# A decoder layer on one core: output projection with five matmuls a chunk, summed by VectorE, and a reordered opening

## The chip, the cores and the metric

The kernel is one launch on one core of a Trainium2 chip. Its time is the device time of that core in microseconds (us); smaller is better. A core has TensorE (PE, matmuls, with a weight load, PEld, beside each), VectorE (DVE), ScalarE (ACT), GpSimd (POOL) and SyncE (SP, which here only issues DMAs). Each engine takes its instructions in order, and they wait for each other by semaphores.

## The reference

One layer for 512 prompt tokens and 8 x 4 sample tokens, 544 tokens in all, width 2048:

```python
def _combine(x, a, p, ga, gb, w_out, ln_g, ln_b):
    mixed = jnp.concatenate([a.reshape(B, T, ATTN_WIDTH) * jax.nn.silu(ga), p * jax.nn.silu(gb)], axis=-1)
    h = (DEEPNORM_ALPHA * x + jnp.einsum('btc,cd->btd', mixed, w_out)).astype(jnp.float32)
    mu = jnp.mean(h, axis=-1, keepdims=True)
    var = jnp.mean(jnp.square(h - mu), axis=-1, keepdims=True)
    y = (h - mu) * lax.rsqrt(var + LN_EPS) * ln_g.astype(jnp.float32) + ln_b.astype(jnp.float32)
```

Ahead of it one input projection (7248 columns) feeds an indexer that picks the keys, sparse attention `a` for prompt and samples (those over paged caches), and a causal pooling mixer `p`. Everything is float32.

## The kernel before, in words

**Projections.** A float32 product is made from float32r parts: activations are kept as `actH` (rounded) and `actL` (the rest), weights as `wH` and `wL`. ScalarE makes a high part by a copy (`high`), GpSimd the low part by a subtraction (`low`). A tile is 128 output columns, its weights come in two units of 8 chunks (128 rows each) through 4 slots. For each chunk TensorE (`unit`, L1157 to L1175) does wH x actH, wH x actL and wL x actH, each for two halves of 272 tokens in two PSUM banks: six matmuls, and a weight load for each. A tile lies in `acc[0]` or `acc[1]`, two banks each; ScalarE copies it to SBUF (`acc_copied` counts that).

**Opening.** x comes by four DMAs of 1 MB (SP issues tokens 0 to 255, ScalarE the rest and the 32 sample rows). TensorE transposes each token tile in four quarters through four PSUM banks, ScalarE writes `actH` from a bank (L718), VectorE `actL` (L1782). After all five tiles, the 80 columns for the indexer's key and weights are projected (tile 0), then eight query tiles of the indexer from `TILE_A` on.

**Middle.** Value, gate, key and query tiles with the prompt's attention, then four rounds (`group`) in which pooling channels are projected while the samples' keys and values pass through. SP's queue is an order written out by hand. `pool_loads` brings the history rows (`hist`) and `w_pool`, `mask` the list of dropped keys into `probS`, `value_page` and `key_unit` the cache pages. `history` on TensorE transposes `hist`, `probs_turned` the softmaxed `probS`.

**Output projection.** 16 tiles from `TILE_D` on. The first (`first_tile`, L1509) is interleaved with the end of the last round. Tiles 1 to 11 are `unit` again, the last four are done in two parts (`out_part`, 288 and 256 tokens, one matmul per product). When a tile is done and copied to `raw`, `rows` (L1675) transposes it into two banks `yp` and `ys`, in the middle of the next tile. VectorE then adds alpha x + bank into `y` (`residual`), takes statistics and multiplies by `ln_g`. `y` is filled with x by five DMAs, issued once the last attention output has left its bank; behind them in the same queue comes `ln_g` for all partitions. On VectorE the statement ahead of the loop over tiles is: `memset gb`, which waits for all of `y`, then a wait for `ln_g`.

Of the kernel before, what the change touches and what calls it, by code (L numbers as in the profile page):

```python
# [32 lines left out]
P = 128  # L33
D = 2048
KC = D // P
# [49 lines left out]
LATE_T = 2 * P  # L85
EARLY_COLS, LATE_COLS = slice(LATE_T, T), slice(0, LATE_T)
# [24 lines left out]
def tile_turn(tile, i=None, per=0):  # L111
# [8 lines left out]
    return Turn(slot, n if i is None else i * step + n)  # L120

# [53 lines left out]
def layer_program(nc, x_prompt, x_sample, cache_k, cache_v, cache_kidx, state_pool, page_table,  # L175
# [4 lines left out]
    with ctx:  # L180
# [10 lines left out]
        actH = sb("actH", [P, KC, T], F32R)  # L191
        actL = sb("actL", [P, KC, T], F32R)
# [121 lines left out]
        acc_copied = sems("acc_copied", 2)  # L314
        bank_full = {j: sem(f"bank_full{j}") for j in (*four, OUT, SIDE)}
# [63 lines left out]
        xb = banks.stage([f"x{t}{q}" for t in range(TT + 1) for q in range(4)], four)  # L379
# [69 lines left out]
        def _(sp):  # L449
# [15 lines left out]
            sp.dma_start(pageT[:], page_table.rearrange("(a b) c -> a (b c)", a=1)).then_inc(pages_in, 16)  # L465
            sp.dma_start(s_pool[0, :, 0:HIST - NT, :], state_pool[0, :, NT:HIST, :]).then_inc(spool_sent, 16)
# [16 lines left out]
            with sp.Fori(0, 4) as i:  # L483
                for j in range(2):
                    load_tile(w_view, QI0 + (2 * i + j) * P, TILE_A + j, i, 2)

                    for q in range(4):
                        b = xb(f"x{TT}{q}")
                        sp.wait_ge(bank_free[b.slot], b.read)
                    for p in range(BESIDE):  # L490
                        index_page(2 * BESIDE * i + (BESIDE * j + p))
            for j in range(2):
                load_tile(w_view, V0 + j * P, TILE_C + j)
            with sp.Fori(8 * BESIDE, NB * PAGES) as at:
                index_page(at)
# [97 lines left out]
            pool_loads(0)  # L593
# [82 lines left out]
        def _(act):  # L676
# [17 lines left out]

            def halves(ap):
                return ap.rearrange("p (a t) -> p a t", a=2)
# [9 lines left out]
            act.dma_start(headrot[:], head_rot).then_inc(consts_in, 16)  # L706
            act.dma_start(halfscale[:], pool_scale[0].rearrange("(j p) -> p j", p=P), allow_slow_non_contiguous=True).then_inc(consts_in, 16)


            for t in range(TT + 1):  # L710
                if t == TT:
                    for half in range(2):
                        high(0, half, width=KW)
# [7 lines left out]
            for q in range(4):  # L721
                b = xb(f"x{TT}{q}")
                act.wait_ge(bank_free[b.slot], b.read)
            act.dma_start(irot[:], idx_rot).then_inc(irot_in, 16)

# [3 lines left out]
            src, copied = projected(0)  # L729
            act.activation(halves(wiT[ID:KW, :]), src[ID:KW], ACT.Copy, scale=ISCALE)  # L730
            act.activation(halves(kiT[0:ID, :]), src[0:ID], ACT.Copy).then_inc(copied, 1)
# [366 lines left out]
            with act.Fori(0, 5) as i:  # L1098
                for j in range(2):
                    high(TILE_D + j + 2, 0, i, 2)  # L1100
                    src, copied = projected(TILE_D + j, i, 2)
                    act.activation(halves(raw[:, j]), src, ACT.Copy).then_inc(copied, 1)
                    high(TILE_D + j + 2, 1, i, 2)

            def out_copy(n):
                src, copied = projected(TILE_D + n)
                if n < WHOLE:
                    act.activation(halves(raw[:, n % 2]), src, ACT.Copy).then_inc(copied, 1)
# [26 lines left out]
        def _(pe):  # L1135

            for s in (*stage_ready, *stage_free, *acc_copied, *bank_free.values(), *v_free):
                pe.sem_inc(s, 1)
# [1258 lines left out]
```

## Time and profile before

| | us |
|---|---|
| timed runs | 1153.33, 1153.55, 1156.03 (median 1153.55) |
| profiled execution, its own time | 1152.01 |
| its span, first to last instruction | 1150.2 |
| TensorE busy in the span | 1123.2 |
| VectorE, ScalarE, GpSimd busy | 641.5, 327.1, 372.8 |

The span begins with the first instruction, and all moments below count from there. "Idle before" in a row is the time that the engine stood still ahead of the group, and the arrow names what ended it. Matmuls overlap: the distance between starts is what one costs, not its own duration. PEclk 1.00 is full speed (2.4 GHz), 0.50 the lower level (1.2 GHz).

### The profile page before, as it was taken

What the parts mean: (1) busy time and instruction counts of PE and PEld (TensorE: products, weight loads), DVE (VectorE), ACT (ScalarE), POOL (GpSimd) and SP (SyncE); (2) the same over time, 40 slices, a digit from 0 to 9 for tenths busy, and PEclk for the clock granted to TensorE, in tenths of its full rate; (3) what the DMA queues carried; (4) which work ended last, traced back from release to release, by engine and by line L of the source; (5) the groups of instructions that cost most, each with busy time, mean ns of one, the idle gap of its engine ahead of it and who ended that gap; (6) DMA issues with size and microseconds to landing.
All of it is one profiled execution on the core that took longest, in us unless ns stands there. A gap on an engine that the chain in (4) does not pass through costs nothing.

```text
span 1150.2 us, 29683 instructions
## 1 busy us (share of the span) xinstructions
PE 1123.2 (98%) x11836; PEld 1046.7 (91%) x11836; DVE 641.5 (56%) x1184; ACT 327.1 (28%) x605; POOL 372.8 (32%) x158
## 2 busy tenths in 40 slices
PE   6999999999999999999999999999999999999996
PEld 5988889999999999999999898988889889999994
DVE  3566666897547456654266564565546443233356
ACT  5233234323332322332233221221212332121340
POOL 2332332233234333333431313221322233433570
PEclk9999999999999999999999999999999999999997
DMA  8543232333233233335323888887978785232333
GB/s 261 137 108 88 61 100 70 83 93 93 74 91 90 82 86 93 89 83 167 111 66 110 274 318 294 303 284 266 336 240 300 224 284 142 73 91 80 106 108 156
DMA packets 208039, 175.86 MB, mean 153 GB/s; under 512 B 20114, under 2 KB 188874, under 8 KB 206706
## 3 DMA queue, kind: packets, MB, share of 16 engines
q1 hardware_dynamic: 194394, 165.58, 46.7%
q10 hardware_dynamic: 13536, 8.68, 2.5%
q8 instruction: 87, 1.43, 0.5%
q14 instruction: 22, 0.18, 0.0%
HBM read 164.29 MB, written 10.03 MB: 152 GB/s over the span
## 4 chain that ended last, share of the span: by engine, by line
PE 90%; DVE 5%; DMA 1%; issue 1%; SPq 1%; ACT 1%; ACTq 0%; DVEq 0%
PE acc L1173 68%; PE acc L1155 4%; PE acc L1563 3%; PE bank L1494 2%; PE bank L1249 2%; PE bank L1366 2%; PE acc L1616 2%; PE bank L1385 1%; DVE scoreP L1868 1%; DVE top L1864 1%; PE acc L1522 1%; DMA xnat<-in_x_prompt 1%; PE bank L1301 1%; PE bank L1375 1%; DMA hist<-in_state_pool 1%
## 5 line engine op out<-in xcount | busy, mean ns | idle before, releaser
L664 POOL TENSOR_TENSOR wL<-rawW,wH 128x1024 fp32r<-128x1024 f32 (+1 forms) x154 | 372.6, 2421 | 746.7 <-ACT wH L686 746.7
L1173 PE MATMUL acc<-actH,wH 128*128 128x272 f32 (+1 forms) x2168 | 464.2, 295 | 1.2 <-DVE actL L1782 1.2
L1173 PE MATMUL acc<-actH,wL 128*128 128x272 f32 (+1 forms) x2168 | 449.0, 289 | 0.0
L1173 PE MATMUL acc<-actL,wH 128*128 128x272 f32 (+1 forms) x2168 | 447.7, 288 | 0.0
L1173 PEld LDWEIGHTS acc<-actH,wH 128*128 128x128 f32 (+1 forms) x2168 | 339.3, 188 | 31.3 <-issue 29.6
L1173 PEld LDWEIGHTS acc<-actL,wH 128*128 128x128 f32 (+1 forms) x2168 | 340.4, 188 | 0.0
L1173 PEld LDWEIGHTS acc<-actH,wL 128*128 128x128 f32 (+1 forms) x2168 | 338.5, 188 | 0.0
L686 ACT ACTIVATE wH<-rawW 128x1024 fp32r<-128x1024 f32 (+1 forms) x154 | 161.7, 1054 | 262.1 <-PE acc L1173 232.5
L1820 DVE SCALAR_TENSOR_TENSOR scoreP<-relu,wiN,scoreP 128x256 f32<-128x256 f32 (+2 forms) x54 | 45.3, 878 | 33.4 <-ACT relu L743 33.4
L1973 DVE STREAM_TRANSPOSE kPage<-kPage 128x1024 f32<-128x1024 f32 x30 | 37.1, 1238 | 38.2 <-DMA kPage<-in_cache_k 37.4
L2216 DVE SCALAR_TENSOR_TENSOR y<-y,bank 128x512 f32 x12 | 8.2, 688 | 89.8 <-PE bank L1683 86.7
L2030 DVE SCALAR_TENSOR_TENSOR mixed<-bank,gate 128x128 f32<-128x128 f32 x32 | 9.3, 289 | 68.3 <-PE bank L1385 68.3
L743 ACT ACTIVATE relu<-bank 128x512 f32<-128x512 f32 (+3 forms) x63 | 28.9, 502 | 57.8 <-PE bank L1249 34.7
L1905 DVE MAX8 top<-scoreS 32x8 f32<-32x1056 f32 x32 | 39.9, 1247 | 3.1
L1908 DVE MATCH_REPLACE8 scoreS<-top,scoreS 32x1056 f32<-32x1056 f32 x32 | 39.4, 1231 | 0.0
L1563 PE MATMUL acc<-vPage,probST 128*4 128x128 f32 x1024 | 38.5, 273 | 0.4 <-issue 0.4
L1155 PE MATMUL acc<-actH,wH 128*128 128x288 f32 (+1 forms) x128 | 37.8, 295 | 0.0
L1155 PE MATMUL acc<-actL,wH 128*128 128x288 f32 (+1 forms) x128 | 36.9, 288 | 0.0
L1155 PE MATMUL acc<-actH,wL 128*128 128x288 f32 (+1 forms) x128 | 36.8, 287 | 0.0
L1974 DVE STREAM_TRANSPOSE kPage<-kPage 128x1024 f32<-128x1024 f32 x30 | 36.1, 1202 | 0.0
L1494 PE MATMUL bank<-kPage,qBlock 128*32 128x64 f32 x1920 | 33.2, 220 | 0.5 <-issue 0.4
L1563 PEld LDWEIGHTS acc<-vPage,probST 128*4 128x4 f32 x1024 | 23.0, 86 | 10.2 <-issue 8.2
(232 smaller groups left out, 1083.6 us busy)
## 6 DMA issues: line engine op xcount, KB each, us to landing
rawW<-in_w_in SPq DMA_DIRECT2D x112, 512.0 KB, 3.9
vPage<-in_cache_v SPq DMA_DIRECT2D x64, 512.0 KB, 6.7
kPage<-in_cache_k SPq DMA_DIRECT2D x60, 512.0 KB, 5.1
rawW<-in_w_out SPq DMA_DIRECT2D x40, 512.0 KB, 3.9
y<-in_x_prompt SPq DMA_DIRECT2D x4, 1024.0 KB, 7.9
out_y_prompt<-y SPq DMA_DIRECT2D x8, 512.0 KB, 2.6
xnat<-in_x_prompt SPq DMA_DIRECT2D x2, 1024.0 KB, 7.7
xnat<-in_x_prompt ACTq DMA_DIRECT2D x2, 1024.0 KB, 11.4
```

The costliest lines, as they stand in the source:

```text
L664: pool.tensor_tensor(wL[:, slot, :, 0:width], rawW[:, slot, :, 0:width], wH[:, slot, :, 0:width].bitcast(F32), ALU.subtract).then_inc(stag ...
L686: act.activation(wH[:, t.slot, :, 0:width], rawW[:, t.slot, :, 0:width], ACT.Copy).then_inc(high_ready[t.slot], 1)
L743: act.activation(relu[0:rows, t.slot, 0:n], src[0:rows, 0:n], ACT.Relu).then_inc(relu_full[t.slot], 1)
L1155: last = pe.matmul(acc[t.slot][:, e, 0:cols.stop - cols.start], w[:, u.slot, k, :], a[:, (1 - half) * HU + k, cols], start=(half == 0 and ...
L1173: last = pe.matmul(acc[t.slot][0:width, e, 0:HT], w[:, u.slot, k, 0:width], a[:, kk, e * HT:(e + 1) * HT], start=(half == 0 and k == 0 and ...
L1494: last = pe.matmul(bank[b.slot][j * SPAN:(j + 1) * SPAN, at:at + w], qBlock[:, q:q + SPAN], keys[:, :, row:row + STREAK], start=(a == 0 an ...
L1563: return pe.matmul(bank[o.slot][j * SPAN:j * SPAN + NT, a * P:(a + 1) * P], probs, values, start=start and a == 0, stop=stop and a == HALF ...
L1820: dve.scalar_tensor_tensor(sc, relu[:, r.slot, 0:(t + 1) * P], wiN[:, t - 1, ds(h, 1)], sc, ALU.mult, ALU.add).then_inc(bank_free[b.slot], 1)
L1905: own.step(dve.max(top, scores))
L1908: own.step(dve.match_replace(scores, top, scores, PICKED))
L1973: dve.transpose(parts[0], parts[0])
L1974: dve.transpose(parts[1], parts[1]).then_inc(k_turned, 1)
```

## The change

1. `actH` and `actL` become two halves of one tensor `act_parts` (low first). Tiles 0 to 11 of the output projection take five matmuls a chunk: wH against [low | high] part of tokens 0 to 255 at once (512 columns, a whole bank), wL against the high part (256 columns, added to the bank's second half), and three of 288 columns for the other tokens in the other bank. The sum of the bank's two halves is the result. ScalarE copies the second half and the rest, VectorE adds the first half in SBUF (`joint_sum`), and `rows` waits for that add (`acc_summed`).
2. Opening: x2, the sample rows and x3 are issued after x0 has landed; `headrot` and `halfscale` move behind the splits; tokens are turned in the order 0, 1, 2, samples, 3, and the 80-column tile is done for tokens 0 to 255 first (256 columns) and then for the rest (288). SP loads the first two query tiles as soon as x3 is in and ahead of the index pages; the copy of the old pool state moves behind them.
3. `pool_loads(0)` moves ahead of `unit(5)`.

```diff
+        act_parts = sb("act_parts", [P, 2, KC, T], F32R)
+        actL, actH = act_parts[:, 0], act_parts[:, 1]
...
+            def joint_products(slot, u, k, kk, first, last, parts=(0, 1)):
+                main = acc[slot][:, 0, JOINT:2 * JOINT]
+                both = acc[slot][:, 0, :].rearrange("p (a t) -> p a t", a=2)
+                high, low = w_slot(wH, u, k), w_slot(wL, u, k)
+                if 0 in parts:
+                    if first:
+                        end = pe.matmul(both, high, act_parts[:, :, kk, 0:JOINT], start=True, stop=False)
+                    end = pe.matmul(main, low, actH[:, kk, 0:JOINT], start=False, stop=False)
+                    if not first:
+                        end = pe.matmul(both, high, act_parts[:, :, kk, 0:JOINT], start=False, stop=last)
+                if 1 in parts:
+                    rest = acc[slot][:, 1, 0:T - JOINT]
+                    pe.matmul(rest, high, actH[:, kk, JOINT:T], start=first, stop=False)
+                    pe.matmul(rest, high, actL[:, kk, JOINT:T], start=False, stop=False)
+                    end = pe.matmul(rest, low, actH[:, kk, JOINT:T], start=False, stop=last)
...
             def rows(j, i):
-                copied(TILE_D + j, i, 2)
+                summed(TILE_D + j, i, 2)
...
             dve.memset(gb[:], 0.0).then_inc(gb_clear, 1)
             dve.wait_ge(ln_in, 16)
+            def joint_sum(j, i):
+                t, s = tile_turn(TILE_D + j, i, 2), joint_turn(TILE_D + j, i, 2)
+                dve.wait_ge(acc_copied[t.slot], t.read)
+                dve.tensor_tensor(raw[:, j, 0:JOINT], acc[t.slot][:, 0, 0:JOINT], raw[:, j, 0:JOINT], ALU.add
+                                  ).then_inc(acc_summed[s.slot], 1)
...
                 for j in range(2):
+                    joint_sum(j, i)
                     residual(2 * i + j, j, i)
...
             for side in MASK_HERE:
                 for a in range(HALF):
                     sp.dma_start(dropD[:, side, a, :, :], dropS[:, side, :]).then_inc(drop_out, 16)
+            pool_loads(0)
             unit(5)
             sp.wait_ge(c_done, 1)
             for p in range(3):
                 value_page(0, p)
             mask(0, None)
             key_unit(1, 0, TAKEN.index(0) + 1)
-            pool_loads(0)
...
             act.dma_start(sq[:], square).then_inc(square_in, 16)
-            for t in range(2, TT):
-                act.dma_start(xnat[:, t, :], x_prompt[0, t * P:(t + 1) * P, :]).then_inc(x_in[t], 16)
+            act.dma_start(pageT[:], page_table.rearrange("(a b) c -> a (b c)", a=1)).then_inc(pages_in, 16)
+            act.wait_ge(x_in[0], 16)
+            act.dma_start(xnat[:, 2, :], x_prompt[0, 2 * P:3 * P, :]).then_inc(x_in[2], 16)
             act.dma_start(xnatS[:], x_sample.rearrange("b t d -> (b t) d")).then_inc(xs_in, 16)
+            act.dma_start(xnat[:, 3, :], x_prompt[0, 3 * P:4 * P, :]).then_inc(x_in[3], 16)
...
+            for t in TURNED[:4]:
+                x_turned(t)
+            index_part(0, 0)
+            x_turned(TURNED[4])
+            index_part(0, 1)
+            index_part(1, 0)
+            index_part(1, 1)
```

Where the output projection's loop begins on VectorE, before:

```order
L2205 MEMSET shift 128x640
L2207 MEMSET shift 128x20 [waits dve_steps]
L2209 MEMSET gb 128x512 [waits y_in]
L2237 UNCONDITIONAL_BRANCH [waits ln_in]
L2237 ISA
L2216 ISA [waits bank_full4]
L2216 SCALAR_TENSOR_TENSOR y<-y,bank 128x4x128
```

and now (L2297 is `joint_sum`; `acc_copied1` is ScalarE's copy of the first tile):

```order
L2286 MEMSET shift 128x640
L2288 MEMSET shift 128x20 [waits dve_steps]
L2290 MEMSET gb 128x512 [waits y_in]
L2325 UNCONDITIONAL_BRANCH [waits ln_in]
L2325 ISA
L2297 TENSOR_TENSOR raw<-acc,raw 128x256 [waits acc_copied1]
```

The add stands behind both waits and ahead of the first `residual`. On TensorE, in the middle of the second tile, the end of its first unit and the transposes of the first tile, before:

```order
L1173 MATMUL acc<-actL,wH 128x272 x2
L1173 MATMUL acc<-actH,wL 128x272 x2
L1208 REGISTER_ALU
L1199 REGISTER_ALU [waits acc_copied1]
L1683 MATMUL bank<-sq,raw 128x128 [waits bank_free4]
L1683 MATMUL bank<-sq,raw 128x128 x3
```

and now:

```order
L1240 MATMUL acc<-act_parts,wH 128x288
L1241 MATMUL acc<-act_parts,wL 128x288
L1224 REGISTER_ALU
L1260 REGISTER_ALU [waits acc_summed1]
L1764 MATMUL bank<-sq,raw 128x128 [waits bank_free4]
L1764 MATMUL bank<-sq,raw 128x128 x3
```

The transposes stand where they stood; they wait for `acc_summed1`, VectorE's add, in place of the copy. On ScalarE at the start of the program, before:

```order
L702 DMA sq<-const_square 128x288
L704 DMA xnat<-in_x_prompt 128x2048 x2
L705 DMA xnatS<-in_x_sample 32x2048
L706 DMA headrot<-const_head_rot 32x1088
L707 DMA halfscale<-in_pool_scale 128x8x1
L718 ACT_TABLE_LOAD
L718 ACTIVATE actH<-bank 128x4x128 [waits bank_full4]
```

and now:

```order
L722 DMA sq<-const_square 128x288
L723 DMA pageT<-in_page_table 1x64
L725 DMA xnat<-in_x_prompt 128x2048 [waits x_in0]
L726 DMA xnatS<-in_x_sample 32x2048
L727 DMA xnat<-in_x_prompt 128x2048
L737 ACT_TABLE_LOAD
L737 ACTIVATE act_parts<-bank 128x4x128 [waits bank_full4]
```

Three DMA issues and the table load stand behind the wait for x0, ahead of the first split.

## Rows read from the trace of the kernel before

**Rows 1.** The page: busy us (share of the span) and instructions; the chain by engine.
```profile
PE 1123.2 (98%) x11836; PEld 1046.7 (91%) x11836; DVE 641.5 (56%) x1184; ACT 327.1 (28%) x605; POOL 372.8 (32%) x158
PE 90%; DVE 5%; DMA 1%; issue 1%; SPq 1%; ACT 1%; ACTq 0%; DVEq 0%
```

**Rows 2.** Windows of the opening: stretch, us, busy by engine, PEclk, DMA share, GB/s.
```profile
17.90:21.30 3.40, 1.82 (x18) 1.28 (x16) 2.69 (x8) 2.67 (x8) 1.94 (x2) 0.99 0.32 87
21.30:24.70 3.40, 3.35 (x15) 3.38 (x16) 0.00 (x0) 1.06 (x1) 1.49 (x2) 0.51 1.16 326
```

**Rows 3.** Timeline of the opening: start, us, engine, line, out<-in, count, [idle before].
```profile
4.29 1.28 ACT L718 ACT_TABLE_LOAD   x1 [4.29 <-issue]
6.64 3.67 PE L1223 MATMUL bank<-sq,xnat 128*128 128x128 f32 x16 [6.64 <-DMA sq<-const_square]
7.79 0.60 ACT L718 ACTIVATE actH<-bank 128x512 fp32r<-128x512 f32 x1 [2.21 <-PE bank L1223]
11.12 1.97 PE L1223 MATMUL bank<-sq,xnat 128*128 128x128 f32 x16 [0.81 <-DMA xnat<-in_x_prompt]
...
12.44 7.26 DVE L1782 TENSOR_TENSOR actL<-bank,actH 128x512 fp32r<-128x512 f32 x12 [0.77 <-ACT actH L718]
...
18.56 1.35 ACT L686 ACTIVATE wH<-rawW 128x640 fp32r<-128x640 f32 x2
...
19.36 3.05 POOL L664 TENSOR_TENSOR wL<-rawW,wH 128x640 fp32r<-128x640 f32 x2 [18.94 <-ACT wH L686]
...
21.35 0.71 PE L1173 MATMUL acc<-actH,wH 128*80 128x272 f32 x2 [1.16 <-DVE actL L1782]
...
34.84 0.41 PE L1173 MATMUL acc<-actH,wH 128*128 128x272 f32 x2
```

**Rows 4.** Timeline at the first history load and the mask, VectorE and TensorE.
```profile
641.22 0.46 DVE L1994 CUSTOM_DVE_ANT_0 probS<-bank,probS 128x288 f32<-128x288 f32 x1 [6.81 <-DMA probS<-dropD]
...
644.96 1.93 DVE L2005 TENSOR_SCALAR probS<-probS,stat 128x288 f32<-128x288 f32 x1
...
644.93 0.29 PE L1598 MATMUL acc<-sq,hist 120*128 120x120 f32 x1 [1.04 <-DMA hist<-in_state_pool]
...
648.16 0.76 PE L1550 MATMUL bank<-sq,probS 128*32 128x32 f32 x64
```

**Rows 5.** The chain in the output projection: start, us, matmuls in a train.
```profile
945.10 12.02 PE acc L1173 x96
...
1080.61 6.39 PE acc L1155 x48
...
1107.14 5.66 PE acc L1155 x48
```

**Rows 6.** Timeline where attention ends and the output projection begins.
```profile
934.29 1.98 SPq L629 DMA_DIRECT2D y<-in_x_prompt  x4
...
936.83 0.45 SPq L632 DMA_DIRECT2D mixed<-in_ln_g  x1
...
944.39 0.60 PE L1683 MATMUL bank<-sq,raw 128*128 128x128 f32 x4
...
948.42 0.48 DVE L2209 MEMSET gb<- 128x512 f32 x1 [12.84 <-DMA y<-in_x_sample]
951.98 0.69 DVE L2216 SCALAR_TENSOR_TENSOR y<-y,bank 128x512 f32 x1 [3.07 <-DMA mixed<-in_ln_g]
```

**Rows 7.** A tile in the middle of the loop, and a VectorE line of 128x256.
```profile
1051.76 0.62 ACT L1102 ACTIVATE raw<-acc 128x544 f32<-128x544 f32 x1 [5.43 <-PE acc L1173]
...
1057.57 0.60 PE L1683 MATMUL bank<-sq,raw 128*128 128x128 f32 x4
...
1058.33 0.69 DVE L2216 SCALAR_TENSOR_TENSOR y<-y,bank 128x512 f32 x1 [8.80 <-PE bank L1683]
...
L2258 DVE SCALAR_TENSOR_TENSOR y<-y,bank 128x256 f32<-128x256 f32 x8 | 3.3, 410 | 7.6 <-PE bank L1705 7.6
```

**Rows 8.** Window from the y loads to the first transposes.
```profile
936.00:944.39 8.39, 8.39 (x69) 8.39 (x68) 0.00 (x0) 1.57 (x2) 4.44 (x2) 1.00 0.99 417
```

More of the change, by code:

```diff
@@ L120, in tile_turn, with joint_turn @@
     return Turn(slot, n if i is None else i * step + n)
+def joint_turn(tile, i=None, per=0):
+    n = (tile - TILE_D) // 2
+    return Turn(tile % 2, n if i is None else i * (per // 2) + n)
 class Banks:
@@ L693, in projected, with joint_projected @@
                 return acc[t.slot][:, :, 0:HT], acc_copied[t.slot]
+            def joint_projected(tile, i=None, per=0):
+                t = tile_turn(tile, i, per)
+                act.wait_ge(tile_ready[t.slot], t.full)
+                return acc[t.slot][:].rearrange("p e t -> p (e t)")[:, JOINT:JOINT + T], acc_copied[t.slot]
             def halves(ap):
@@ L1195, in unit_chunks, with summed, joint_unit, w_slot @@
                     last.then_inc(tile_ready[t.slot] if half else stage_free[u.slot // 2], 1)
+            def summed(tile, i=None, per=0):
+                t = joint_turn(tile, i, per)
+                pe.wait_ge(acc_summed[t.slot], t.read)
+            def joint_products(slot, u, k, kk, first, last, parts=(0, 1)):
[13 more added lines that the diff above has]
+                    end = pe.matmul(rest, low, actH[:, kk, JOINT:T], start=False, stop=last)
+                return end
+            def joint_unit(tile, half, i=None, per=0):
+                t, u, s = tile_turn(tile, i, per), turn(2 * tile + half, 4, i, 2 * per), joint_turn(tile, i, per)
+                pe.wait_ge(stage_ready[u.slot], u.read)
+                if half == 0:
+                    pe.wait_ge(acc_copied[t.slot], t.free)
+                    pe.wait_ge(acc_summed[s.slot], s.free)
+                for k in range(HU):
+                    end = joint_products(t.slot, u.slot, k, (1 - half) * HU + k, half == 0 and k == 0, half == 1 and k == HU - 1)
+                end.then_inc(tile_ready[t.slot] if half else stage_free[u.slot // 2], 1)
+            def w_slot(w, u, k):
+                return w[:, u, k, :]
             def take(b):
@@ L1211, in _, with x_turned @@
             pe.wait_ge(square_in, 16)
-            for t in range(TT + 1):
+            def x_turned(t):
                 n = P if t < TT else NS
@@ L1225, in _, with x_split, index_part @@
                     full(b, last)
-            for q in range(4):
-                b = xb(f"x{TT}{q}")
+            def x_split(t, q):
+                b = xb(f"x{t}{q}")
                 pe.wait_ge(bank_free[b.slot], b.read)
-            for half in range(2):
-                unit(0, half, width=KW)
+            def index_part(e, half):
+                cols = slice(0, FIRST_T) if e == 0 else slice(FIRST_T, T)
+                dst = kiwi[0:KW, cols]
+                slot, read = half, turn(half, 4).read
+                pe.wait_ge(high_ready[slot], 1)
+                for w, parts in ((wH, (actH, actL)), (wL, (actH,))):
+                    if w is wL:
+                        pe.wait_ge(stage_ready[slot], read)
+                    for k in range(HU):
+                        if k % 4 == 0 and w is wH:
+                            x_split(1 if e == 0 else 3, 2 * half + k // 4)
+                        for a in parts:
+                            last = pe.matmul(dst, w[:, slot, k, 0:KW], a[:, half * HU + k, cols],
+                                             start=(half == 0 and k == 0 and w is wH and a is actH),
+                                             stop=(half == 1 and k == HU - 1 and w is wL))
+                if e == 1:
+                    last.then_inc(stage_free[0] if half == 0 else tile_ready[0], 1)
+            for t in TURNED[:4]:
[5 more added lines that the diff above has]
+            index_part(1, 1)
             def index_weights_turned():
@@ L1518, in first_tile @@
                     pe.wait_ge(mix_low, k - HU + 1 if k >= HU else LATE if parts == (1,) else HU + k + 1)
-                    for w, values in ((wH, (actH, actL)), (wL, (actH,))):
-                        for a in values:
-                            for e in parts:
-                                last = pe.matmul(acc[t.slot][:, e, 0:HT], w[:, u.slot, k % HU, :],
-                                                 a[:, k, e * HT:(e + 1) * HT], start=(k == HU and w is wH and a is actH),
-                                                 stop=(k == HU - 1 and w is wL))
+                    last = joint_products(t.slot, u.slot, k % HU, k, k == HU, k == HU - 1, parts)
                 if chunks[-1] == KC - 1:
@@ L1774, in _ @@
             n = 0
-            for t in range(TT + 1):
+            for t in TURNED:
                 m = P if t < TT else NS
```

67 lines of the change are left out of this document (38 added, 29 removed).

## The prediction

> **What bounds the kernel now.** I read the page's busy table and its chain first. TensorE is busy for 1123.2 us of a span of 1150.2, and 90% of the chain that ended last is TensorE's own work [rows 1]. So an edit pays only if it shortens TensorE's instruction stream or one of the few places where TensorE stands still, and an edit costs whatever new standstill it makes. The windows and the timeline of the opening came next [rows 2, 3], then the timeline where the token history is loaded [rows 4], then the matmul trains of the chain in the output projection [rows 5], and last the moment where attention ends and the output projection begins [rows 6]. There the reader should see one thing: VectorE stands still from 935.6 to 951.98 us, first for the reload of x into `y`, then for `ln_g`, and TensorE doesn't mind, because all it does with VectorE in that time is to fill a bank and go on.
>
> **Part 1, five matmuls in place of six.** Columns don't change: before 6 x 272 = 1632 a chunk, now 512 + 256 + 3 x 288 = 1632. What counts is what a matmul costs beside its columns. Three trains of the chain give it [rows 5]: 272 columns take 12.02 us / 96 = 125.2 ns, 288 take 6.39 / 48 = 133.1, 256 take 5.66 / 48 = 117.9. Per column that is 0.460, 0.462 and 0.461 ns. Over one column per tick of 2.4 GHz the three lie 11.9, 13.1 and 11.2 ns. No train here has 512 columns in this format, so I bound it. If cost is proportional to columns, the 512 take 235.7 ns and a chunk 235.7 + 117.9 + 3 x 133.1 = 752.9 against 751.2 before: nothing. If some 12 ns are a fixed price of each matmul, one of six goes: -12 ns x 16 chunks x 12 tiles = -2.3 us. If the long matmul also lost all its excess (213.3 ns), -22.4 + 1.7 = -20.7 ns a chunk, -4.0 us. A straight line through the outer two points (0.475 ns a column, -3.7 ns at zero) makes the 512 cost 239.5: +5.5 ns a chunk, +1.1 us. I take 0, the nearest rows being proportional; ends -4.0 and +1.1.
>
> The Trainium skill (TensorE: Matmul & The Clock Gate, "Wait — 56ns, not 53.3ns?") says that a warm matmul costs its columns over 2.4 GHz and about 2.5 ns whatever its length. By that rule one matmul fewer gives 2.5 ns x 192 = 0.5 us. The trace disagrees in size: the excess over the columns here is 11 to 13 ns and grows with the length.
>
> The other costs of this part are off the path once the loop runs. Each of 12 tiles gets a VectorE add of 128x256 with one operand in PSUM; the nearest row of that shape takes 410 ns [rows 7]. In the middle of the loop ScalarE copies a tile from 1051.76 to 1052.38, the add would end near 1052.9, and the tile's transposes start only at 1057.57; VectorE sat idle for 8.80 us before it took them up at 1058.33 [rows 7]. Hidden, with 4.7 us of cover.
>
> **Part 2, the new wait.** Before, the transposes of a tile (`rows`) waited for ScalarE's copy. Now they wait for VectorE's `joint_sum`. VectorE is in order, and the first `joint_sum` stands behind `memset gb` (waits for all of `y`) and the wait for `ln_g`. The loads themselves don't move: the `y` loads are issued at 934.29, with the same bytes. TensorE reaches `rows` of the first tile at 944.39; VectorE passes the `ln_g` wait at 951.98 [rows 6]. Add 0.41 us for the sum and about 0.1 for the signal: TensorE goes on at 952.5. Queued behind on TensorE is the whole rest of the output projection, which it did without a stop. The stall is 952.5 - 944.4 = 8.1 us, and nothing later can give it back, since TensorE has no later idle time to shorten except in the tail that follows it. The order before it holds the same columns, so it arrives neither earlier nor later relative to the `y` loads, to some 0.1 us. Bounds: 7.3 us (add and signal at nothing, transfers a few per cent faster) to 9 us (transfers at 0.9 of their rate: 417 GB/s were moved from 936.00 to 944.39 [rows 8]).
>
> The stall also takes the clock. From 17.90 to 21.30 TensorE was busy only 1.82 us, and it then ran at the lower of its two levels (1.2 in place of 2.4 GHz, granted 0.51) from 21.30 to 24.70 [rows 2], with 15 matmuls where full speed gives 27: 1.6 us lost. At the very start, after idleness, 16 transposes took 3.67 us where the next 16 took 1.97 [rows 3]: 1.7 lost. After 8 idle us I add 1.7; ends 0.8 and 3.4. The Trainium skill (same page, "HAM oscillation — how this bites in real kernels") names just this against such a change: a TensorE that waits for a DMA between trains of matmuls restarts at half clock. It would put the same sign on the term; the size above is from the rows.
>
> **Part 3, the opening.** Before, all x is transposed and split, paced by ScalarE and VectorE (12 splits in 7.26 us, 0.605 each), then ScalarE makes the high parts of the 80-column weights at 18.56, and TensorE's first product starts at 21.35; the first 128-column tile starts at 34.84 [rows 3]. Now the products of tokens 0 to 255 may start once x0, x1, x2 and the sample rows are transposed and the first half of the weights has landed. But a step that moves counts whole: ScalarE's table load (at 4.29, behind nothing) now stands behind three DMA issues, which wait for x0. x0 lands by about 6.6 (TensorE starts on it at 6.64), the three issues take some 1.5 us, the table load 1.28: the first split is near 9.3 in place of 7.79. Twelve splits at 0.605 end near 17.2 to 17.9, then the high part 0.7: TensorE's products start near 18.3. From there it is dense: 48 x 117.9 ns = 5.7, sixteen transposes of x3 2.0, 48 x 133.1 = 6.4, end 32.4. GpSimd's low part (half of 3.05 us) is covered by 16 high products (1.9 us), and the split of x3 (four at 0.6 after the transposes) by the second 2.8 us of products. 34.84 - 32.4 = 2.4 us gained, with the half-clock stretch of 21.3 to 24.7 gone since TensorE is dense by then. Ends: 4.2 (splits not held up) and 0 (a half-clock stretch stays, weights land late). The loads of the first query tiles are issued once x3 is in, earlier than before, and cost nothing; the index pages move behind them and are wanted only after the eighth query tile.
>
> **Part 4, the history load.** `pool_loads(0)` moves up in SP's queue, ahead of a weight unit, three value pages, the mask and two key pages. TensorE waited 1.04 us for `hist` at 644.93 [rows 4]; that goes. What is late next is the mask: VectorE waited 6.81 us for it and went on at 641.22, its softmax ends at 646.89, and TensorE's transposes of the result start at 648.16, 1.27 us of slack [rows 4]. The wait saved eats 1.0 us of it, and three DMA issues with 0.37 MB ahead of the mask push it back by 0.6 to 1.8 us. So the gain is 0.7 down to a loss of 0.5, and I take 0.
>
> **The sum**, against the profiled execution's own 1152.0 us (span 1150.2): 0 + 8.1 + 1.7 - 2.4 + 0 = +7.4, that is 1159.4. That execution lies 1.5 us under the median of the three timed runs (1153.55), so the timed median should be near 1160.5 to 1161. I say 1160.5.
>
> **Rivals.**
> B, the clock costs double: the stall's half-clock stretch is the long one (3.4) and the opening keeps its own (gain 0.7 in place of 2.4). For it speaks that the opening still has waits for x3's splits; against it that TensorE is dense from 18.3. +11 us: 1164.
> C, the long matmul sheds its excess: -4.0 for part 1. For it: an excess per matmul exists at all. Against it: three lengths show it proportional [rows 5]. +3.4 us: 1156.5 to 1157.
> D, not slower: the new wait is covered, since `y` and `ln_g` have landed when TensorE gets to `rows`. Then stall and clock term both go and the opening's gain stays: 1152.0 - 2.4 = 1149.6, timed 1151. It decides from the point where 5.4 MB (x whole and `ln_g` for 128 partitions) arrive within the 10.1 us from 934.3, 535 GB/s; the trace shows 417 there [rows 8]. Also under D: something that I take for a wait is passed early.
>
> **Chances.** A (forecast, 1157.5 to 1163) 0.75; B 0.09; C 0.08; D 0.08. About 0.3% (3.5 us) is what a measurement of this kernel tells from no change. A and B and a third of C end above 1157.0, with a little of A below it: slower 0.85. C's rest, most of D: same 0.11. D together with a gain in part 1: faster 0.04. Range for 8 in 10: from 1155 (C, with the better end of the opening) to 1165 (B).
>
> **What the new profile would show.** For part 2: a TensorE idle gap of about 8 us just after the first half unit of the output projection, released by VectorE's add, behind the DMA of `ln_g`; granted clock near half for some us behind it. For part 1: a mean start-to-start of the five near 752.9 ns a chunk. For part 3: the first 128-column product near 32.4 and the first split near 9.3. For part 4: no wait at the history transpose, a short one at the softmax transposes. I am wrong if that gap is under 4 us, or if a chunk takes under 735 ns.

## The result, and the profile after

Seven runs of each kernel: before 1154.08 us (1151.98 to 1156.03), after 1160.79 us (1156.40 to 1163.15). The ratio after to before is 1.0054 [1.0037, 1.0071]: slower by 6.2 us [4.3, 8.2]. Predicted were 1160.5 us, in a range of 1155 to 1165. The profiled execution of after is its fastest run: 1156.40 us with a span of 1154.4. The trace therefore shows less than the runs (+4.4 against before's profiled 1152.01), and the places below are read from it one by one.

The page after: busy us and instructions, and the chain by engine, answering to [rows 1]:

```profile
PE 1123.0 (97%) x11644; PEld 1038.1 (90%) x11644; DVE 647.4 (56%) x1196; ACT 326.3 (28%) x605; POOL 373.0 (32%) x158
PE 91%; DVE 5%; DMA 2%; issue 1%; SPq 0%; ACT 0%; DVEq 0%; ACTq 0%
```

TensorE does the same 1123 us of work in a longer span, and the DMA share of the chain has gone from 1% to 2%. Of TensorE's waits (line waited for: us in total, times, longest) the one at the top is new:

```profile
PE bank L1764 <- DVE raw L2297: 6.6, 1, 6.6
```

The timeline where the output projection begins (start, us, engine, line, out<-in, count, [idle before]), answering to [rows 6]:

```profile
932.68 0.45 SPq L646 DMA_DIRECT2D mixed<-in_ln_g  x1
...
944.12 0.48 DVE L2290 MEMSET gb<- 128x512 f32 x1 [12.74 <-DMA y<-in_x_sample]
946.45 0.42 DVE L2297 TENSOR_TENSOR raw<-acc,raw 128x256 f32<-128x256 f32 x1 [1.84 <-DMA mixed<-in_ln_g]
...
947.00 1.11 PE L1764 MATMUL bank<-sq,raw 128*128 128x128 f32 x4 [6.62 <-DVE raw L2297]
948.29 0.69 DVE L2304 SCALAR_TENSOR_TENSOR y<-y,bank 128x512 f32 x1 [1.42 <-PE bank L1764]
...
956.58 0.42 DVE L2297 TENSOR_TENSOR raw<-acc,raw 128x256 f32<-128x256 f32 x1 [5.20 <-ACT raw L1123]
```

Read it from below: TensorE's four transposes at 947.00 stood idle for 6.62 us behind VectorE's add; the add at 946.45 stood behind the DMA of `ln_g`; and the fill ahead of it behind the last part of `y`. The second tile's add (956.58) waits only for ScalarE's copy and holds nobody up. The same stretch in windows (stretch, us, busy by engine, PEclk, DMA share, GB/s), answering to [rows 8]:

```profile
936.00:940.40 4.40, 4.38 (x30) 3.88 (x28) 0.00 (x0) 0.00 (x1) 2.39 (x1) 1.00 1.02 430
940.40:944.90 4.50, 0.00 (x0) 0.00 (x0) 0.48 (x1) 1.06 (x1) 2.34 (x1) 0.99 1.02 355
944.90:951.70 6.80, 4.70 (x18) 4.35 (x19) 3.23 (x10) 0.00 (x0) 0.00 (x0) 0.50 0.51 152
951.70:960.00 8.30, 8.30 (x57) 7.83 (x57) 0.42 (x1) 1.57 (x2) 2.40 (x1) 1.00 0.38 93
```

In the second window TensorE does nothing, in the third it has restarted but is granted half its clock until 951.70, and in the fourth it is back at full speed.

The opening, answering to [rows 3]:

```profile
7.42 1.28 ACT L737 ACT_TABLE_LOAD   x1 [7.42 <-issue]
8.71 4.46 ACT L737 ACTIVATE act_parts<-bank 128x512 fp32r<-128x512 f32 x8
...
13.12 1.97 PE L1285 MATMUL bank<-sq,xnat 128*128 128x128 f32 x16 [0.58 <-DMA xnat<-in_x_prompt]
...
15.73 0.76 ACT L700 ACTIVATE wH<-rawW 128x640 fp32r<-128x640 f32 x1
...
17.34 2.11 PE L1306 MATMUL acc<-act_parts,wH 128*80 128x256 f32 x16
...
24.80 2.27 PE L1306 MATMUL acc<-act_parts,wH 128*80 128x288 f32 x16
...
31.12 0.66 PE L1197 MATMUL acc<-act_parts,wH 128*128 128x272 f32 x4
```

and its two windows, answering to [rows 2]:

```profile
17.90:21.30 3.40, 3.40 (x32) 3.40 (x31) 0.15 (x1) 0.89 (x2) 1.79 (x2) 1.00 0.99 266
21.30:24.70 3.40, 3.40 (x32) 3.40 (x31) 2.48 (x4) 1.63 (x4) 0.00 (x0) 1.00 1.20 290
```

The products start at 17.34 in place of 21.35, TensorE is dense in both windows, and the half-clock stretch is gone from this trace. The history and the softmax, answering to [rows 4]:

```profile
640.72 0.27 PE L1679 MATMUL acc<-sq,hist 120*128 120x120 f32 x1
...
642.92 1.92 DVE L2086 TENSOR_SCALAR probS<-probS,stat 128x288 f32<-128x288 f32 x1
...
644.95 0.75 PE L1631 MATMUL bank<-sq,probS 128*32 128x32 f32 x64 [0.95 <-issue]
```

The wait for `hist` is gone, and TensorE now stands 0.95 us ahead of the softmax transposes, which it starts 0.11 us after the softmax has ended (642.92 + 1.92 = 644.84). Last, the chain in the output projection, answering to [rows 5]: the start of the transposes of two tiles, eight tiles apart.

```profile
974.39 0.44 PE bank L1764 x4
...
1074.58 0.44 PE bank L1764 x4
```

(1074.58 - 974.39) / 8 = 12.52 us a tile. Before, the trains of [rows 5] with the transposes between them made 12.58 us.

Where the profiled difference arises, as how far after's trace lies from before's at each place:

| place | before | after | after - before |
|---|---|---|---|
| first 128-column product | 34.84 | 31.12 | -3.72 |
| history transpose | 644.93 | 640.72 | -4.21 |
| softmax transposes | 648.16 | 644.95 | -3.21 |
| last transpose of the attention output | 933.65 | 929.44 | -4.21 |
| transposes of the first output tile | 944.39 | 947.00 | +2.61 |
| of the second | 956.95 | 961.69 | +4.74 |
| of the eleventh | 1070.16 | 1074.42 | +4.26 |
| end of the span | 1150.17 | 1154.41 | +4.24 |

Two steps go up, both at the new wait: 6.8 us to the first transposes, 2.1 to the second, 9.0 together. The rest gives 4.7 back.

### The profile page after: what moved, and what is told of

It is laid out like the page before. It is cut to its first block, busy times and chain, and to the rows that moved or that the text cites. A ratio compares the mean times of both kernels' runs of the same rounds, so it can differ in the third digit from the quotient of the medians.

```text
span 1154.4 us, 29301 instructions
## 1 busy us (share of the span) xinstructions
PE 1123.0 (97%) x11644; PEld 1038.1 (90%) x11644; DVE 647.4 (56%) x1196; ACT 326.3 (28%) x605; POOL 373.0 (32%) x158
## 4 chain that ended last, share of the span: by engine, by line
PE 91%; DVE 5%; DMA 2%; issue 1%; SPq 0%; ACT 0%; DVEq 0%; ACTq 0%
PE acc L1197 55%; PE acc L1179 4%; PE acc L1236 3%; PE acc L1644 3%; PE bank L1580 3%; PE bank L1335 2%; PE acc L1239 2%; PE acc L1240 2%; PE acc L1241 2%; PE acc L1234 2%; PE bank L1452 2%; PE bank L1471 2%; PE acc L1697 2%; DVE scoreP L1949 1%; DMA mixed<-in_ln_g 1%
## 5 line engine op out<-in xcount | busy, mean ns | idle before, releaser
L1197 PE MATMUL acc<-act_parts,wH 128*128 128x272 f32 x3568 | 605.7, 292 | 0.0
L1197 PEld LDWEIGHTS acc<-act_parts,wH 128*128 128x128 f32 x3568 | 503.5, 188 | 30.0 <-issue 29.6
L1197 PE MATMUL acc<-act_parts,wL 128*128 128x272 f32 x1784 | 369.5, 288 | 0.6 <-issue 0.6
L1197 PEld LDWEIGHTS acc<-act_parts,wL 128*128 128x128 f32 x1784 | 278.7, 189 | 0.5 <-issue 0.5
L1236 PE MATMUL acc<-act_parts,wH 128*128 128x512 f32 x180 | 71.1, 397 | 0.0
L1901 DVE SCALAR_TENSOR_TENSOR scoreP<-relu,wiN,scoreP 128x256 f32<-128x256 f32 (+2 forms) x54 | 45.3, 878 | 33.4 <-ACT relu L764 33.4
L1239 PE MATMUL acc<-act_parts,wH 128*128 128x288 f32 x192 | 57.1, 298 | 0.0
L1240 PE MATMUL acc<-act_parts,wH 128*128 128x288 f32 x192 | 57.0, 297 | 0.0
L1241 PE MATMUL acc<-act_parts,wL 128*128 128x288 f32 x192 | 56.9, 296 | 0.0
L2054 DVE STREAM_TRANSPOSE kPage<-kPage 128x1024 f32<-128x1024 f32 x30 | 37.1, 1237 | 34.3 <-DMA kPage<-in_cache_k 33.4
L1234 PE MATMUL acc<-act_parts,wL 128*128 128x256 f32 x192 | 55.5, 289 | 0.0
L1179 PE MATMUL acc<-act_parts,wH 128*128 128x288 f32 (+1 forms) x256 | 49.6, 292 | 0.0
L1240 PEld LDWEIGHTS acc<-act_parts,wH 128*128 128x128 f32 x192 | 36.4, 190 | 7.5
L1179 PEld LDWEIGHTS acc<-act_parts,wH 128*128 128x128 f32 x256 | 40.1, 188 | 2.4 <-issue 2.3
```

The source lines that it names most:

```text
L1179: last = pe.matmul(acc[t.slot][:, e, 0:cols.stop - cols.start], w[:, u.slot, k, :], a[:, (1 - half) * HU + k, cols], start=(half == 0 and ...
L1197: last = pe.matmul(acc[t.slot][0:width, e, 0:HT], w[:, u.slot, k, 0:width], a[:, kk, e * HT:(e + 1) * HT], start=(half == 0 and k == 0 and ...
L1234: end = pe.matmul(main, low, actH[:, kk, 0:JOINT], start=False, stop=False)
L1236: end = pe.matmul(both, high, act_parts[:, :, kk, 0:JOINT], start=False, stop=last)
L1239: pe.matmul(rest, high, actH[:, kk, JOINT:T], start=first, stop=False)
L1240: pe.matmul(rest, high, actL[:, kk, JOINT:T], start=False, stop=False)
```

## The experiments

Ratios are to the kernel before on the same chip, with a 95% interval; 0.001 is 1.15 us. "The place" is the stretch from the last transpose of the attention output to the transposes of the second output tile. It takes 23.30 us in the trace of before.

**1. The wait alone, on the old kernel.** Six matmuls, old opening, old history; only the transposes wait for a 5-column fill that VectorE does where the add would stand:

```diff
             def rows(j, i):
-                copied(TILE_D + j, i, 2)
+                summed(TILE_D + j, i, 2)
...
+            def joint_sum(j, i):
...
+                dve.wait_ge(acc_copied[t.slot], t.read)
+                dve.memset(std[:], 0.0
+                                  ).then_inc(acc_summed[s.slot], 1)
...
                 for j in range(2):
+                    joint_sum(j, i)
                     residual(2 * i + j, j, i)
```

> The kernel before, six matmuls, old opening, with the new wait alone: the transposes of a tile wait for a VectorE instruction (a memset of 5 columns in the place of the add) that stands where the add stands. My theory: a gap of 7 to 8 us at the first transposes, then some us at half clock; 1154 + 7.5 + 2 = 1163 us, ratio 1.007 to 1.010. Rival (spread loss): a gap that a faster stretch afterwards gives back, time within 0.3% of before.

Measured: 1164.26 us in four runs, ratio 1.0100 [1.0085, 1.0114]. Its timeline:

```profile
952.44 0.06 DVE L2234 MEMSET std<- 128x5 f32 x1 [1.85 <-DMA mixed<-in_ln_g]
...
952.63 1.11 PE L1701 MATMUL bank<-sq,raw 128*128 128x128 f32 x4 [6.41 <-DVE std L2234]
```

An instruction of 0.06 us costs 11.5 us. The length of the add (0.42 us in after) is a small part of the price; nearly all of it is the add's place in VectorE's order. In the trace the place takes 32.61 us, 9.3 more than before, while the span is 11.0 longer: the other 1.7 us arose ahead of it, where the edit changes nothing that TensorE waits for (the first 128-column product is at 35.78 in place of 34.84). So the trace gives 9.3 for the wait itself, a little under the timed interval. The windows of its restart (columns as above) show half clock well past the gap:

```profile
951.80:955.20 3.40, 2.57 (x12) 2.51 (x13) 1.19 (x5) 0.00 (x0) 0.00 (x0) 0.50 0.08 21
955.20:958.60 3.40, 3.40 (x17) 3.40 (x17) 1.68 (x7) 0.00 (x0) 0.00 (x0) 0.51 0.96 273
958.60:962.00 3.40, 3.40 (x29) 3.40 (x29) 0.00 (x0) 0.00 (x0) 0.00 (x0) 1.00 0.72 180
```

**2. The changed kernel with the add ahead of both waits.**

```diff
-            dve.wait_ge(y_in, 16 * (TT + 1))
             dve.memset(gb[:], 0.0).then_inc(gb_clear, 1)
-            dve.wait_ge(ln_in, 16)
...
                     joint_sum(j, i)
+                    if j == 0:
+                        dve.wait_ge(y_in, 16 * (TT + 1))
                     residual(2 * i + j, j, i)
                     statistics(2 * i + j)
+                    if j == 0:
+                        dve.wait_ge(ln_in, 16)
                     gained(2 * i + j)
```

> The changed kernel with VectorE's order altered in one place: `memset gb` waits for nothing, the wait for `y` stands behind the first add, the wait for `ln_g` behind the first statistics. My theory (the new wait costs a stall and half-clock time, 9 to 10 us together, the rest of the change gains 2.4 or more): no TensorE gap over 1 us at the first transposes of the output projection, no half-clock stretch there, time 1150 to 1152 us, ratio to before 0.996 to 0.999. Rival (the loss is spread over the tiles by the adds and the longer matmuls): the gap goes but the time stays near 1158 to 1160.

Measured: 1150.63 us, ratio 0.9975 [0.9965, 0.9986]. TensorE and VectorE in its timeline:

```profile
942.14 0.60 PE L1764 MATMUL bank<-sq,raw 128*128 128x128 f32 x4
...
946.18 0.69 DVE L2302 SCALAR_TENSOR_TENSOR y<-y,bank 128x512 f32 x1 [8.75 <-DMA y<-in_x_sample]
...
948.47 0.69 DVE L2319 TENSOR_TENSOR y<-y,mixed  x1 [0.21 <-DMA mixed<-in_ln_g]
```

VectorE waits for `y` as before (8.75 us), and TensorE passes without a stop at 942.14, since only the residual is behind that wait. The place takes 23.34 us, what it took before. So the loss is the wait and nothing else in the change, and without it the change is a small gain. The edit does one thing more: the fill that SyncE's queue waits for no longer waits itself, so the next weight load is issued 6.5 us after the last transpose of the attention output in place of 18.0 in after. The place shows no gain from that.

**3. One of the two waits put behind the add.** The wait for `ln_g` goes behind the first statistics, the fill that waits for `y` stays ahead:

```diff
             dve.memset(gb[:], 0.0).then_inc(gb_clear, 1)
-            dve.wait_ge(ln_in, 16)
...
                     statistics(2 * i + j)
+                    if j == 0:
+                        dve.wait_ge(ln_in, 16)
```

> The changed kernel with the wait for `ln_g` behind the first statistics, but the wait for `y` still ahead of the first add. My theory: the gap ends when the last bytes of x are in, at about 945.2 instead of 947.0 in the profile, so it is 4.8 us instead of 6.6; with the clock the same, 1.8 to 3.1 us less than the changed kernel, 1158 to 1159 us. Rival (only being idle counts, not how long): unchanged, 1161.

Measured: 1157.65 us, ratio 1.0038 [1.0024, 1.0052]. Waits of TensorE:

```profile
PE bank L1764 <- DVE raw L2296: 4.8, 1, 4.8
```

6.6 became 4.8 us: `y` makes up 4.8 of the stall and `ln_g` the last 1.8. The second tile's transposes came 14.14 us after the first's. It is a price of two waits in a row, and half a repair gives back only the last part. That is shown by the trace; the timed ratio is lower than in after by 0.0016 and than in the repeat by 0.0004, both within the intervals, and doesn't decide it.

**4. The gap filled with work, to separate clock and stall.** 72 spare transposes run on TensorE just ahead of the loop over tiles, the waits stay:

```diff
+            spare = take(yb("yp0"))
+            for n in range(72):
+                pe.transpose(spare[:, 0:P], ident, ident)
             with pe.Fori(0, 5) as i:
```

> The changed kernel with 72 needless 128-column transposes on TensorE between the first tile of the output projection and the second (about 7.8 us of work at 109 ns each, written to a bank that is overwritten later). My theory (the loss is idle time plus what the clock loses behind it): TensorE no longer idles at the first transposes, the granted clock stays at 1.00 there, the tile after takes 12.52 us instead of 14.69, and the time falls by what the clock cost, 2 to 3 us, to about 1158 us; the idle 6.6 us are only replaced by work. Rival (the clock loses nothing that the time shows): 1161 to 1162, since the filling is longer than the wait. Rival (something else than the wait holds the loop): the filling comes on top, 1168.

Measured: 1160.25 us, ratio 1.0060 [1.0043, 1.0077]: no faster than after, so the time that was expected is a miss. Its windows say why:

```profile
948.80:952.20 3.40, 3.40 (x24) 3.15 (x22) 0.48 (x1) 0.00 (x0) 0.00 (x0) 1.00 0.32 120
952.20:955.60 3.40, 3.03 (x22) 2.70 (x21) 2.29 (x8) 1.06 (x1) 1.98 (x1) 1.00 0.25 64
```

The clock stays at full speed, the second tile follows the first after 12.59 us, and so the 2.1 us of the clock term are gone. But the first transposes come 8.4 us later than without the wait, where the stall had cost 6.8. The filling alone doesn't explain that, because TensorE still stood still behind it:

```profile
952.20 0.43 DVE L2300 TENSOR_TENSOR raw<-acc,raw 128x256 f32<-128x256 f32 x1 [1.79 <-DMA mixed<-in_ln_g]
...
952.76 0.65 PE L1764 MATMUL bank<-sq,raw 128*128 128x128 f32 x4 [0.37 <-DVE raw L2300]
```

The add began 18.6 us after the last transpose of the attention output, in after 17.0: `ln_g` came later here, and a shorter filling would only have waited longer for it. That the half clock follows from the idle stretch is shown, a saving from filling it isn't.

**5. Five matmuls alone,** with the wait out of the way, old opening and old history (the edit is experiment 2's, with the other two parts undone):

> The kernel before with the five matmuls and the VectorE adds but the old opening and the old place of the history load, and with the waits for `y` and `ln_g` behind the first add, as in the run above. Proportional cost (what I took): same as before, a tile every 12.56 us. A fixed 2.5 ns a matmul: 12.52 us a tile, 0.5 us less in all. A fixed 12 ns: 12.37 us a tile, 2.3 us less. Rival (spread loss): over 12.7 us a tile, 1 to 3 us more than before.

Measured: 1153.85 us, ratio 1.0003 [0.9994, 1.0011]: nothing, to 1.2 us either way. Its trace has the same 12.52 us a tile as after, which is the second of the three figures expected.

**6. The opening alone,** on the kernel before:

> The kernel before with the reordered opening alone. From the changed kernel's profile (first 128-column product at 31.1 us in place of 34.8): 3.7 us less than before if all of it reaches the end, ratio 0.997; 2.4 by my forecast. Rival: the gain is lost again on the way (the kernel waits for a load that is as late as before), ratio 1.000.

Measured: 1152.68 us, ratio 0.9986 [0.9977, 0.9996]: 1.6 us faster [0.5, 2.7], which excludes both the 3.7 us and the rival's nothing. The first 128-column product is at 31.59.

**7. The history load alone,** `pool_loads(0)` ahead of `unit(5)` in the kernel before:

> The kernel before with the earlier history load alone. My forecast: no wait at the history transpose, a wait of 0 to 1 us at the softmax transposes in its place, 0 (-0.7 to +0.5) us, ratio 1.000. What the sum of the parts leaves over (changed kernel without the wait 1150.6, five matmuls alone 1153.9, opening alone 1152.7, before 1154.0: 1.9 us) would be a rival: 2 us less, ratio 0.998.

Measured: 1155.28 us, ratio 1.0020 [1.0007, 1.0033]: slower by 2.3 us where no change was expected. The wait for `hist` is gone from its trace too, but that trace is of its fastest run (1152.14 us, span 1150.3) and shows no place where 2 us were lost. Experiments 10 and 11 test it again.

**8. Is the opening held by ScalarE's table load?** Experiment 2 with a copy of one column ahead of the wait for x0, so that the table is loaded before:

```diff
+            act.wait_ge(square_in, 16)
+            act.activation(stat[:, 31:32], sq[:, 0:1], ACT.Copy)
             act.wait_ge(x_in[0], 16)
```

> The changed kernel with the waits for `y` and `ln_g` behind the first add, and with ScalarE's table load ahead of its wait for x0 (a one-column copy placed there). My theory: the table load (1.28 us) was on the opening's path, so the first split starts at 7.6 to 7.9 us instead of 8.7 and the first 128-column product up to 1 us earlier than with the waits moved alone; 1149 to 1150.6 us. Rival (the opening is held by the arrival of x2 and of the weights): the first split is earlier, the first 128-column product is not, 1150.6.

Measured: 1150.44 us, ratio 0.9975 [0.9961, 0.9989], the same as experiment 2. Its timeline:

```profile
7.82 1.25 ACT L739 ACTIVATE act_parts<-bank 128x512 fp32r<-128x512 f32 x2 [1.18 <-PE bank L1287]
...
13.72 1.97 PE L1287 MATMUL bank<-sq,xnat 128*128 128x128 f32 x16 [1.76 <-DMA xnat<-in_x_prompt]
```

The first split is 1.0 us earlier than in experiment 2 (8.81), and TensorE still waits 1.76 us for x2, whose load is issued only when x0 has landed. The table load is off the path; x2's arrival is on it. The first 128-column product is 0.8 us earlier too (31.73 against 32.56), but so is x2 (its transposes start at 13.72 against 14.56), though the copy put its issue off by 0.3 us. In the nine traces with the new opening x2's transposes start anywhere from 13.1 to 14.6, so this can't be put down to the edit.

**9. The changed kernel again,** for the size of the loss on the same chip as experiments 10 and 11:

> The changed kernel once more. Its seven timed runs lie between 1156.4 and 1163.2 us, and the profiled one is the fastest. My theory: the cost of the wait varies from run to run with the arrival of `ln_g` and with how long the clock stays low behind the gap; median 1160 to 1161.5, and a profile with a gap of 6 to 8 us and 3.4 to 7 us at half clock behind it. Rival: the first seven runs were a poor sample, median 1158 to 1159, near what the profile's ledger gives (9.0 us for the wait).

Measured: 1159.85 us, ratio 1.0042 [1.0027, 1.0057]. That is just under the range expected, and above the rival's. Its timeline has the same gap:

```profile
946.72 0.42 DVE L2297 TENSOR_TENSOR raw<-acc,raw 128x256 f32<-128x256 f32 x1 [1.86 <-DMA mixed<-in_ln_g]
...
947.27 1.11 PE L1764 MATMUL bank<-sq,raw 128*128 128x128 f32 x4 [6.92 <-DVE raw L2297]
```

**10. Five matmuls and the opening, waits behind the add, history in its old place:**

> Five matmuls and the new opening, waits for `y` and `ln_g` behind the first add, history load in its old place. Parts alone: opening -1.4 us, five matmuls -0.2, history +1.3; all three together (waits moved) -3.4. If parts add up: about 1152.4. If the history load costs here what it cost alone: 1.3 us less than with it, 1149.3. If it gains or loses nothing in this company: 1150.6.

Measured: 1150.47 us, ratio 0.9967 [0.9956, 0.9978]. Against the kernel before on the same chip (1154.72) that is -3.8 us [-5.1, -2.5]; the three figures expected were named against 1154.0, as -1.6, -4.7 and -3.4. The sum of the parts is excluded, the other two aren't told apart.

**11. Opening and history, six matmuls:**

> The kernel before with the new opening and the earlier history load, six matmuls. If parts add up: -1.4 + 1.3, 1153.9. If the history load gains beside a shorter opening what it lost alone: 1151 to 1152.

Measured: 1152.43 us, ratio 0.9983 [0.9971, 0.9994], or -2.0 us [-3.3, -0.7]. The sum of the parts (-0.1) is excluded; the other figure (-2 to -3) isn't.

Against experiment 6 (0.9986) the history adds nothing in 11; against experiment 10 (0.9967) it costs 0.9 us in 2, within the intervals. The 2.3 us of experiment 7 don't come back, so the part is worth nothing, or a loss too small to tell.

The lowest ratio is that of experiment 10: 0.9967, faster than before by 3.8 us [2.5, 5.1] and than after by 9 to 10 us. Experiments 2 and 8 are within its interval, so it isn't shown to be better than they are.

| kernel | ratio | the place, us (before 23.30) |
|---|---|---|
| after; again | 1.0054; 1.0042 | 32.25; 32.60 |
| wait alone | 1.0100 | 32.61 |
| gap filled | 1.0060 | 31.76 |
| wait for `y` alone ahead | 1.0038 | 29.91 |
| add ahead of both | 0.9975 | 23.34 |

## Why the prediction was right

**The mechanism (part 2) is shown, from both sides.** Added to the old kernel the wait costs 11.5 us [9.8, 13.2] (experiment 1); taken from the new one it gives back 9.1 us, by the ratios of after and experiment 2 (7.7 with the repeat). Forecast were 8.1 + 1.7 = 9.8. The traces give 9.0 for after and 9.3 for the wait alone and for the repeat. It was found by reading VectorE's idle time before a wait that cost nothing, and asking who would stand behind it next.

**Its two terms were off in opposite directions.** The stall was forecast at 8.1 us (7.3 to 9) and came out below the lower bound: 6.6, 6.4 and 6.9 us in three traces. The step that failed is that `ln_g` comes when it came before, "VectorE passes the `ln_g` wait at 951.98". Counted from the last transpose of the attention output (the mark), VectorE passes it after 18.3 us in before [rows 6], but after 17.0, 17.1 and 17.3 us in after, in experiment 1 and in the repeat. The rest, 0.2 us, is that TensorE reached the transposes 10.95 in place of 10.74 us after the mark.

That is not the scatter of one trace. In the three other traces with six matmuls in which TensorE goes on (experiments 6, 7 and 11) VectorE passes after 18.8, 18.5 and 18.6 us. What sets them apart stands in the DMA view of the 17 us behind the mark (queue and kind: packets, MB, share of 16 engines), in before from 934 to 951 us:

```profile
q1 hardware_dynamic: 776, 5.52, 86.5%
q8 instruction: 1, 0.02, 0.5%
```

and in after from 929.8 to 946.8, where no instruction queue moves anything:

```profile
q1 hardware_dynamic: 778, 5.52, 85.7%
```

The packet of before is 16 KB of instructions. It starts 13.6 us after the mark and takes 1.3 us, while the last of `y` and `ln_g` are on their way. The thirteen traces divide by it without exception: in the eight with an instruction packet 5.0 to 14.2 us after the mark, `ln_g` lands at 18.0 to 19.2 us (16 KB in before and experiments 4, 6, 7, 8, 10 and 11; 8 KB in experiment 5); in the five with none until 16.4 (after, its repeat, experiments 1, 2 and 3), at 16.8 to 17.1. In experiment 1, with six matmuls like before but a TensorE that stands still, the packet comes at 18.5, not at 13.5 to 14.2. So the moment at which a DMA lands was read rightly and didn't carry over: the change, and the stall itself, moved what shares the DMA engines with it. That the packet makes the 1.2 us is read from this order alone; no run varies it by itself.

The clock was forecast at 1.7 (0.8 to 3.4): the second tile came 14.69 (after), 14.72 (repeat) and 15.30 us (experiment 1) after the first, in place of 12.56: 2.1, 2.2 and 2.7. So the smaller stall and the dearer clock partly cancel, 9.0 for 9.8. In after the half-clock stretch began inside the gap, at 944.9, and reached 4.7 us into the work. The Trainium skill (TensorE: Matmul & The Clock Gate, "HAM oscillation — how this bites in real kernels") foretells the sign, a restart at half clock behind a wait for a DMA; the traces agree in every kernel with the gap, and experiment 4 shows that it goes when TensorE is kept busy.

**How much of the hit is luck.** The median, 1160.79 for a forecast of 1160.5, is closer than the working deserves. The slowdown by the ratio is 6.2 us, where 7.4 had been added up, and the profiled execution took 1156.40 us, 3.0 less than the 1159.4 that the sum gave for it. It happened to be the fastest of seven runs, 4.4 under their median, where 1.5 had been allowed.

**Part 1, five matmuls: forecast 0, timed +0.3 us [-0.7, +1.3].** The trace shows -0.06 us a tile, 3 ns a chunk, some -0.6 us in all. I had said 752.9 ns a chunk by proportion. Start to start the 512 columns take 230.5 ns, the 256 take 117.8, the 288 take 133.4, 133.4 and 133.1: 748.2. So rival C, a long matmul that sheds its excess, is right in direction and for a small part: 17 ns of the 22.4 by proportion are left, not none. The Trainium skill's rule (TensorE: Matmul & The Clock Gate, "Wait — 56ns, not 53.3ns?"), a fixed 2.5 ns for each matmul, gives the 3 ns of difference almost exactly, though not the 11 to 17 ns that each matmul here takes beyond its columns.

**Part 3, the opening: forecast -2.4, timed -1.6 [-2.7, -0.5], in after's trace -3.7.** The first 128-column product is at 31.1 to 33.6 in nine traces with the new opening (mean 32.3), and at 33.4 to 36.2 in four with the old (mean 35.1): -2.7. The trace of after has the earliest of the nine. The half clock is not gone from all of them: experiments 3, 4 and 11 have a half-clock stretch of 3.4 us that begins at 18.1 to 18.8, and with 33.62, 32.71 and 33.53 the three latest first products. The size was about right and a step of the reasoning not: I let the splits start late behind the table load and pace everything. In after they are paced so to 13.17, just as x2 lands; in experiments 2 and 8 x2 comes later still and the table load doesn't matter.

**Part 4, the history: forecast 0 (-0.7 to +0.5).** In the trace it went as worked out: the wait of 1.04 us goes, and 1.0 us is lost again before the softmax transposes (-4.21 to -3.21 in the table above), where a wait of 0.95 us stands now. Timed, it is +2.3 alone and 0 to +0.9 beside other parts. What experiment 7 lost isn't explained.

**Rival D** (not slower, the wait covered) fell: VectorE is past `y` and `ln_g` 14.7 and 17.0 us after the mark, TensorE is there after 10.95. **Rival B** (clock double) fell: the clock cost 2.1 to 2.7 us at the stall, not 3.4, and the opening of after kept its gain.

**What stays open.** The parts don't add up exactly. Alone, the five matmuls give +0.3 and the opening -1.6, together -3.8 [-5.1, -2.5] (experiment 10). The stretch from the first 128-column product to the end of attention takes 897.5 to 901.2 us in thirteen traces, whatever the change. A part of that is the clock, in a place that no edit touches. The window there of experiment 6:

```profile
789.00:792.40 3.40, 3.40 (x18) 3.40 (x16) 1.60 (x9) 0.00 (x0) 0.00 (x0) 0.52 0.94 253
```

and of experiment 2:

```profile
789.00:792.40 3.40, 3.40 (x30) 3.40 (x29) 2.82 (x16) 0.90 (x3) 0.00 (x0) 1.00 0.94 282
```

Experiments 3, 4, 6 and 11 are granted half clock for 3.4 us there (18 matmuls in the window above), the other nine traces have no half-clock stretch at that place. All four have the new opening, but so do after, its repeat and experiments 2, 8 and 10, which don't show it. Whether the changed opening moves the chance of it can't be read from one trace of each kernel.

## What to carry to other kernels

A wait on a slack engine is free only as long as nothing that the bound engine needs stands behind it: before giving such an engine a new job, look at what it is idle for at that place, and put the job ahead of the wait. Add to a stall the clock that it costs behind it, and don't take the moment at which a DMA lands for fixed: look at what else used the DMA engines then, and whether the change moves it. More traces alone would not have helped here, since the four traces of kernels with six matmuls and no stall agree. Fewer, longer matmuls with the same columns are worth almost nothing here, and not a new dependency.

## What the runs showed of the hardware

- Start to start, float32r matmuls of 256, 272, 288 and 512 columns take 117.8, 125.2, 133.3 and 230.5 ns. Beyond one column per tick of 2.4 GHz that is 11.1, 11.9, 13.3 and 17.2 ns: neither fixed nor proportional.
- The half-clock stretch at the same gap was 6.8 us (after), 10.2 (experiment 1) and 3.4 (experiment 3). It began ahead of the restart in the first two and just behind it in the third, and cost 2.1, 2.7 and 1.6 us.
- With a packet of instructions (8 or 16 KB) among the loads of `y` and `ln_g`, the last of them landed 18.0 to 19.2 us after the last transpose of the attention output (eight traces), without one 16.8 to 17.1 (five traces). Whether the packet is the cause wasn't tested.
- TensorE's wait for x2, a 1 MB part issued when x0 has landed, was 0.5 to 1.9 us in nine traces with the new opening.
